# Five conditioning sets of a streamed two-network kernel placed beside other weight groups

## The reference, cut to what matters

```python
def mla_branch(...):                                  # first network, each of 2 layers
    q = (rms_norm(c_q, q_a_norm) @ wq_b)...; kv = (rms_norm(c_kv, kv_a_norm) @ wkv_b)...
    o = causal_block_attention(q, k, v)               # its output goes through mla_w_o
def adaln(c, w, b):
    m = jax.nn.silu(c) @ w + b                        # w is 1024 x 6144
    return [t[:, None, :] for t in jnp.split(m, 6, axis=-1)]
def second_block(...):
    for i in range(DEPTH_2):                          # 4 layers
        shift1, scale1, gate1, shift2, scale2, gate2 = adaln(c, ada_w[i], ada_b[i])
        h = x * (1.0 + scale1) + shift1
        y = mixer(h)                                  # i == 2: the matrix memory, h @ ml_w_up first
        x = layer_norm(DN_ALPHA * x + (1.0 + gate1) * y, ...)
        h = x * (1.0 + scale2) + shift2
        y = conv_ffn(h, ...)                          # up projection, convolution, gate, down projection
        x = layer_norm(DN_ALPHA * x + (1.0 + gate2) * y, ...)
```

## Time and profile before

| | |
|---|---|
| median of 3 runs | 2510.39 us |
| span of the profiled execution | 2510.8 us |
| TensorE matmul busy | 2344.0 us, 93% |
| VectorE busy | 1948.0 us, 78% |
| ScalarE busy | 1391.5 us, 55% |
| DMA | 463.36 MB, mean 185 GB/s |
| loads of the stream | 434 of 1 MB, 4.9 us from issue to landing |

### The profile page before, as it was taken

One profiled execution on the slowest core, in us unless ns is written; L12 is line 12 of the kernel. 1 busy time (PEld: TensorE's weight loads), 2 busy tenths in 40 slices (PEclk: granted clock), 3 DMA queues, 4 the chain that ended last, 5 costly groups with the idle time before them and its releaser, 6 DMA issues. The chain is left out here.

```text
span 2510.8 us, 45734 instructions
## 1 busy us (share of the span) xinstructions
PE 2344.0 (93%) x18552; PEld 2234.5 (89%) x18552; DVE 1948.0 (78%) x3439; ACT 1391.5 (55%) x2552; POOL 12.8 (1%) x20
## 2 busy tenths in 40 slices
PE   8899999989999998979998989999988999988998
PEld 7899999978898998879998879998788999867998
DVE  6578798856687986978897868886559889867885
ACT  7635565465365644746645657646554674533764
POOL 0000000000000000000000000000000000000000
PEclk9999999999999999999999999999989999989999
DMA  6215578723164776214575615583424458722552
GB/s 248 89 51 203 184 278 301 311 84 118 51 252 185 286 305 249 101 66 153 188 301 217 235 68 185 191 312 119 176 92 185 163 191 312 273 103 74 195 195 92
DMA packets 64225, 463.36 MB, mean 185 GB/s; under 512 B 7248, under 2 KB 7440, under 8 KB 8208
## 3 DMA queue, kind: packets, MB, share of 16 engines
q1 hardware_dynamic: 64016, 460.44, 49.4%
HBM read 459.37 MB, written 1.05 MB: 183 GB/s over the span
## 5 line engine op out<-in xcount | busy, mean ns | idle before, releaser
L730 PE MATMUL psum<-arena_rounded,upper_rounded 128*128 128x256 f32 (+2 forms) x5112 | 1439.8, 282 | 87.9 <-DVE ring_rounded L571 19.1
L731 PE MATMUL psum<-arena_rounded,upper_rounded 128*128 128x256 f32 (+2 forms) x5112 | 1426.6, 279 | 0.0
L732 PE MATMUL psum<-arena_rounded,ring_rounded 128*128 128x256 f32 (+2 forms) x5112 | 1426.0, 279 | 0.0
L730 PEld LDWEIGHTS psum<-arena_rounded,upper_rounded 128*128 128x128 f32 (+2 forms) x5112 | 969.6, 190 | 109.6 <-issue 69.2
L562 ACT ACTIVATE upper_rounded<-ring 128x1024 fp32r<-128x1024 f32 (+4 forms) x958 | 751.6, 796 | 521.6 <-PE psum L732 426.9
L571 DVE TENSOR_TENSOR ring_rounded<-ring,upper_rounded 128x1024 fp32r<-128x1024 f32 (+4 forms) x958 | 838.8, 897 | 259.3 <-ACT upper_rounded L562 254.4
L731 PEld LDWEIGHTS psum<-arena_rounded,upper_rounded 128*128 128x128 f32 (+2 forms) x5112 | 968.7, 189 | 0.7 <-issue 0.5
L732 PEld LDWEIGHTS psum<-arena_rounded,ring_rounded 128*128 128x128 f32 (+2 forms) x5112 | 969.0, 190 | 0.1
L586 DVE CUSTOM_DVE_ANT_0 ring<-ring,silu_c,cols 128x1024 f32<-128x1024 f32 x192 | 244.7, 1279 | 0.0
L2366 DVE SCALAR_TENSOR_TENSOR arena<-psum,cols,arena 128x255 f32<-128x255 f32 (+1 forms) x352 | 153.2, 477 | 56.8 <-ACT arena L2333 53.7
L2333 ACT ACTIVATE arena<-psum,cols 128x256 f32<-128x256 f32 x176 | 89.5, 561 | 72.9 <-PE psum L732 72.9
(11 more groups left out here) (497 smaller groups left out, 2348.8 us busy)
## 6 DMA issues: line engine op xcount, KB each, us to landing
ring<-stream_dram SPq DMA_DIRECT2D x434, 1024.0 KB, 4.9
const<-const_dram SPq DMA_DIRECT2D x1, 1540.0 KB, 14.6
x<-x_dram SPq DMA_DIRECT2D x1, 1024.0 KB, 4.8
out_dram<-x SPq DMA_DIRECT2D x4, 256.0 KB, 2.0
cols<-cols_dram SPq DMA_DIRECT2D x1, 974.0 KB, 11.3
silu_c<-c_dram SPq DMA_DIRECT2D x1, 512.0 KB, 15.3
const<-const_dram SPq DMA_DIRECT2D x1, 67.0 KB, 4.6
pos<-positions_dram SPq DMA_DIRECT2D x1, 64.0 KB, 5.7
```

The lines of the kernel that those rows point to most:

```text
L730: pe.matmul(out, upper, x[0][:, b.k, :], start=(b.k == 0), stop=False)
L731: pe.matmul(out, upper, x[1][:, b.k, :], start=False, stop=False)
L732: ins = pe.matmul(out, lower, x[0][:, b.k, :], start=False, stop=(b.k == nk - 1))
```

## The change

One set less goes to each down projection but the last one (3 to 2 in the two of the first network, 2 to 1 in three of the second), five in all. One set goes to each of the two `mla_o` groups, two to `ml_x`, and `ml_z` has two where it had one. The count stays 24, the order of the sets too. The quarters of a set in `mla_o` stand 8 blocks apart, at blocks 0, 8, 16 and 24 (`KD` is 8); in all other groups 0.16 of the window is over 8, so that part of the change does nothing there. The number of units, of pieces and of all other instructions is the same.

```diff
@@ with_sides
-            at = int(window * (n + 0.16 * quarter))
+            at = int(window * n + max(KD, 0.16 * window) * quarter)
@@ weight_order
-        g["mla_o", l] = by_rounds(matrix("mla_w_o", (l,), H_MLA * D_V, tiles(0, KD)))
+        g["mla_o", l] = with_sides(by_rounds(matrix("mla_w_o", (l,), H_MLA * D_V, tiles(0, KD))), sides(1))
-        g["down", l] = with_sides(by_rounds(matrix("w_down", (l,), F1, tiles(0, KD))), sides(3))
+        g["down", l] = with_sides(by_rounds(matrix("w_down", (l,), F1, tiles(0, KD))), sides(2))
-            g["ml_x", i] = with_raw(by_rounds(matrix("ml_w_up_2", (0,), D, tiles(0, K_ML)), TOGETHER),
+            g["ml_x", i] = with_raw(with_sides(by_rounds(matrix("ml_w_up_2", (0,), D, tiles(0, K_ML)), TOGETHER), sides(2)),
-            g["ml_z", i] = with_raw(with_sides(by_rounds(matrix("ml_w_up_2", (0,), D, tiles(I_ML, K_ML))), sides(1)),
+            g["ml_z", i] = with_raw(with_sides(by_rounds(matrix("ml_w_up_2", (0,), D, tiles(I_ML, K_ML))), sides(2)),
-                                      sides(2 if i + 1 < L2 else 0))
+                                      sides(1 if i + 1 < L2 else 0))
```

## The result

The kernel after takes 2533.62 us (median of 6 runs, 2532.07 to 2543.5) against 2510.47 us for the kernel before, measured beside it (6 runs, 2504.16 to 2521.7): a ratio of 1.009, with a 95% interval of 1.0063 to 1.0117. Run again later it gave 1.0101 (1.0079 to 1.0124). The change makes the kernel some 23 to 25 us slower. The forecast was 2522.5 with a range up to 2531: the direction was right, the size about half of what it is, and the time lies above the range.

What follows compares the result with a forecast made beforehand. TensorE was taken to bound the kernel, with stops where it waits for VectorE. From the 2510.8 us span, -7.0 + 10.0 + 3.6 + 3.2 + 2.3 = +12.1 gave 2522.9, less 0.4 for the median: 2522.5, range 2509 to 2531.

Steps and rivals of the forecast that it cites:

- attention ahead of `mla_o`, twice: Piece at chunk 4, straight ahead of the third normalising that TensorE waits for: 1.0 us in each of two layers.
- norm ahead of `ml_x`: Two pieces ahead of the last addition to x, 2.4 us, and slower sums of squares, 1.2: together 3.6 us.
- first tiles of `ml_x`: Four pieces ahead of the first convolution start the convolutions 3.7 us late; 3.2 us passes on, between 1.5 and 3.7.
- `ml_z`: Gain of 1.2 us at L3158, loss of 3.5 by four pieces up to L3174: net 2.3, between 0 and 4.
- The relief: Three feed-forward down projections with one set instead of two lose their later stops: 7.0 us won, bounds 0 and 11.6.
- the first stop of each: In each relieved feed-forward down projection the stop from the quarter at block 0 stays, about 1.5 us each.
- rival 2: The down projections do not gain, the 7.0 us is missing: +19.1, about 2529.5 us; chance 0.12.
- The end of `mla_o`: Late unit and VectorE's pieces delay the block's end: 4.0 us per layer, between 1.7 and 5.3.
- The clock behind `mla_o`: A fall to 1.2 GHz at both `mla_o` ends, about 1.2 us or a little more each, left out of the centre.
- The 2525: Time in us by the Trainium skill's clock rule, with both `mla_o` ends costing 2 to 3 us more.
- Rival 3: The clock falls as well: +2 to +5 us, up to 2528; chance 0.1.
- Rival 1: Pieces hidden, relief whole: -4.6, about 2506 us; chance 0.24 within 0.3% of no change, 0.07 faster.

Runs made afterwards that it cites:

- e8: Kernel before with the side units of the three two-set feed-forward down projections at even places, blocks 10 to 150; ratio to before 0.9995.
- e11: e8 with other side-unit places in hg_f, ml_z and sb_qk too, all sets in their groups; 2502.22 us, ratio to before 0.9955.
- e5: Kernel after with useless small matmuls, 7 behind each attention output projection and 12 ahead of the wait at L3091 in ml_z; ratio to before 1.0079.
- after again: Kernel after, unchanged, run again for a second profile; ratio to before 1.0101.
- e4: Kernel before with three sets moved from feed-forward down projections to the two gates groups and the first network's second down projection; ratio to before 1.0026.

## Why the direction was right and the size too small

The time lies above the range, and what failed is first of all a term that the sum left out, the fall of TensorE's clock; the table shows each term.

To compare stages of different executions I took the pace out: from the start-to-start times of the 15336 weight matmuls I subtracted the pace around each (113 or 118 ns), which leaves the stops, slow matmuls and gaps. Each figure is the mean over the profiles with the new places less the mean over those with the old ones (three or four of each; six for the new `mla_o`). The method leaves a few tenths open: profiles at the same pace have 1.5 and 1.4 us less in the second and third of the relieved down projections, where it gives 1.8 and 1.7.

| term | forecast | measured |
|---|---|---|
| three feed-forward down projections | -7.0 | -2.7 -1.8 -1.7 = -6.2 |
| attention ahead of `mla_o`, twice | +2.0 | +0.7 +1.6 = +2.3 |
| `mla_o` and the gap behind it, twice | +8.0 | +2.0 +2.9 and +2.4 +3.0 = +10.3 |
| slow matmuls in `rwkv_a`, twice | left out | +2.1 +2.6 = +4.7 |
| norm ahead of `ml_x` | +3.6 | +4.4 |
| first tiles of `ml_x` | +3.2 | +3.0 |
| `ml_z` | +2.3 | +6.9 |
| sum | +12.1 | +25.4 |

The sum agrees with the measured 23 to 25 us better than it deserves. With the pace taken out, the two whole profiles of after are only some 19 us longer than the two of before: the stages outside the table were, in these executions, some 6 us shorter. How much of the agreement is luck stays open.

**The relief** was nearly right in its size, and right in what stays: the first stop of each. That rules out rival 2. Its cause was one of place: even places from block 10 on remove most of the stops without removing a set (e8, e11). The later stops had to do with late loads, of which the text said little. This line is of the first down projection of before; the others have 9.3 and 1.9 us there, and after has none in any of the three:

```profile
ACT upper_rounded L562 <- DMA ring<-stream_dram: 10.2, 4, 3.8
```

Whether the load or the pieces ended each stop was not tested apart. The cause given for the first stop, the quarter at block 0, is shown in part: with nothing ahead of block 10 the first group still stops at block 22 (1.1 us instead of 1.4), the second keeps one of its two first stops, the third's falls from 1.9 to 0.9.

**The end of `mla_o`** was right to 0.1 us in the profile shown above. In 6 of the 12 `mla_o` groups with the new places the clock was at half in its first 3 us, 1.7 to 1.9 us each; in none of the 12 with the old ones. That is most of the excess over 8.0 (six times 1.8 us in twelve groups, 1.8 for the two layers): TensorE comes out of the attention, which now has a piece more, slow in some executions and not in others. Why, no run shows. The attention's own term is the least certain: its gap is 32.8 to 35.5 us with the old places and 33.6 to 36.2 with the new ones.

**The clock behind `mla_o`** is the first step that failed. The text weighed it and put it at nothing in the sum, "since other waits of TensorE passed without it". Other waits do pass without it: behind the stop of 1.37 us at 1279.47 in before the granted clock is 1.00. But in the profiles it fell in every `rwkv_a` behind a gap of 3.7 or 4.5 us that nothing filled (8 of 8), and cost 2.0 to 2.8 us each, not the 1.2 read off 16 sums of squares: in `rwkv_a` 23 matmuls run slow. The Trainium skill's rule (TensorE: Matmul & The Clock Gate, HAM oscillation), that idle stretches send the engine to half rate and that the work behind starts cold, agrees with the trace here: 0.50 behind 3.71 us. The 2525 that I worked out by it was too low because it was priced by the same wrong row and counted only two places. Rival 3, the clock, is the one that held, and its upper end, +5, was too low as well: 4.7 us at the two `rwkv_a`, 1.8 at the starts of `mla_o` and at least 1.8 in `ml_z`.

**`ml_z`** is the second step that failed, with 4.6 us nearly as large a miss. The gain at L3158 came as forecast. At L3091 the text counted four pieces between L3158 and the end of L3174, 4.8 us, less 1.3 us of VectorE's gaps. Before has one piece there (at 1812.97); after has six, the one that takes its place (at 1827.91) and these:

```profile
1833.40 1.28 DVE L586 CUSTOM_DVE_ANT_0 ring<-ring,silu_c,cols 128x1024 f32<-128x1024 f32 x1
...
1837.55 1.28 DVE L586 CUSTOM_DVE_ANT_0 ring<-ring,silu_c,cols 128x1024 f32<-128x1024 f32 x1
...
1842.10 1.28 DVE L586 CUSTOM_DVE_ANT_0 ring<-ring,silu_c,cols 128x1024 f32<-128x1024 f32 x1
...
1843.30 1.28 DVE L586 CUSTOM_DVE_ANT_0 ring<-ring,silu_c,cols 128x1024 f32<-128x1024 f32 x1
...
1845.38 1.28 DVE L586 CUSTOM_DVE_ANT_0 ring<-ring,silu_c,cols 128x1024 f32<-128x1024 f32 x1
```

So five more and not four, 6.0 us; the wait grew by 4.5, and the gaps took up 1.5, about what the text gave them. The miscount is 1.0 us of the miss. The other 3.6 stand where the clock is low, for which the forecast asked only at `mla_o`: 1.8 in the products at L3085 (1.97 us became 3.76 in the profile; e5 gives it back), some 1.2 in slow matmuls behind them, and 0.6 in the products at L3080, which are slow in some profiles of both kernels. For the last two the clock as the cause is argued, not shown.

**The norm and `ml_x`** were right. The norm's sums of squares were not slow in the first profile, contrary to the text (3.77 us); the stats matmul ahead of them was (1.22 us instead of 0.70). In after again they were slow, as forecast:

```profile
1705.84 5.27 PE L2213 MATMUL psum<-arena,const 128*128 128x256 f32 x16
```

**From the span to the time.** I took the profiled execution of before as 0.4 us above the median. The runs of after show their time 1.9 us above their span, so it was probably 2.3 above, and the forecast ought to have been 2520.6: a small error that hid 2 us of the large one. Rival 1 is out: the unit in `mla_o` was late, the first tiles of `ml_x` cost 3.0 us, and the down projections gave back some 6 us and not 11.6.

**What stays open.** The pace. In the profiles 1700 to 6900 of the 15300 matmuls stand at 118 ns instead of 113, which is worth 8 to 32 us: 15.7 and 18.1 in the two of before, 27.4 and 26.8 in the two of after. It is larger than most effects looked for here. Whether fewer stops make the slow pace likelier, which would explain why e8 showed nothing for 7.5 us of stops won and why e11 gave 11.6 us where its stages show about 20, can't be told from one or two profiles per kernel.

## What to carry to other kernels

Work put by order between two instructions of an engine costs what waits behind that place, whatever the engine's busy share: find, for each place, the next instruction that the bounding engine waits for, and count in the written order how many pieces stand ahead of it: one too few was 1.0 us here. Where side data share a ring with the weights, look for late loads too. Wherever a change makes the matrix engine idle for more than it did, add the price of the clock, read from dense matmuls at half rate behind it, at every such place and not only where one has looked. And before work is moved to another stage, try other places for it in its own: even spacing and a later first quarter took away as many stops as the move did, though it took places in three more groups (e11) before the time showed a gain.

## What the runs showed of the hardware

- The same matmuls (fp32r, 128x128 by 256 columns) run in long stretches at one of two paces, 113 or 118 ns from start to start, both with a granted clock of 1.00: 60.00 or 62.30 us for the 528 of the last down projection, 120.0 or 124.6 for the 1056 of the up projection ahead of it. Which one a group gets differs from execution to execution; the pace changes mostly at stops and gaps.
- Behind 3.7 us of idle time TensorE's granted clock was 0.50 for about 5 us, and 23 matmul records fitted where 42 do at full clock; matmuls of no use in all but 0.7 us of that time held it at 1.00.
- The length of the wait alone did not decide: behind a stop of 1.37 us the granted clock stayed at 1.00 in before (1279.5 to 1284.5), and behind another of 1.37 us in the down projection of e4 it was 0.51 (905.7 to 908.7).
- A wait of 3.06 us of ScalarE for a late load delayed the end of the block by only 1.6 us, as long as no piece stood behind the chunk.
